# Sampled tokens of a hybrid decoder step: state step within attention, experts within the spreading, heads in the partitions

## The chip, the cores and the metric

The kernel runs on one core of a Trainium2 chip. The metric is the device time of one execution in microseconds (us); less is better. The core's engines work at the same time and wait for each other by semaphores: PE (TensorE), DVE (VectorE), ACT (ScalarE), POOL (GpSimd) and SP (SyncE, which here only starts transfers). POOL starts the gathers of rows by index.

## The reference

One decoder layer is computed for 1024 prompt tokens and for 8 sampled tokens. The sampled ones differ from the prompt in two places: each has its own cache of 512 past keys and values, in four pages, and its own recurrent state.

```
n  = rmsnorm(x);  q,k,v,...,gates = n @ w_in
oa = diff_attention(q, k_all, v_all)              # 4 heads; sampled: 512 cached keys and the own one
S  = f * S + (1 - f) outer v;  ob = q . S         # sampled: one step, 4 heads, state 128 x 128
h  = x + (sig(ga) * (oa @ wa) + sig(gb) * (ob @ wb)) @ w_out
# PEER: 8 heads; for each: top 16 of 128 keys twice, top 16 of the sums -> 16 experts
a  = gelu(expert_u[idx] . n2);  h = h + sum(w * a * expert_v[idx]);  y = rmsnorm(h)
```

Of the 16384 experts a token uses 8 x 16 = 128, with 1024 numbers in each of `expert_u` and `expert_v`.

## The kernel before

The tokens are cut in nine tiles, eight of 128 prompt tokens and one of the 8 sampled ones, in three groups, named a_ (tiles 0 and 1), b_ (2 to 4, the middle group) and c_ (5 to 7 and the sampled tile, the last group). A group runs through stages, each a function, and each stage ends with a barrier of all engines: project, attend_prompt, hgrn (the recurrence of the prompt), hgrn_out (its output: squares, norm, gate, transposes), merge and route (choice of experts). The last group has attend_sample between attend_prompt and hgrn. After it come spread (turns the choices of tiles 5 to 7 into dense weight matrices), sample_experts (the experts of the sampled tile, gathered) and dense (all experts for tiles 5 to 7, by matmul). Within a stage each engine has its own program in the written order; nothing reorders it.

Beside the stages of the groups b_ and c_ and of dense runs a side job, `Side`: the experts of tiles 0 to 4, gathered row by row. One "side token" is one of 640 steps: POOL gathers 128 rows of 8 KB (L1568), DVE makes a dot with the rows (L1647) and, two steps later, adds the second half of the rows (L1611); ACT makes the coefficient between (L1587 and L1589). A table, SHARES, says how many steps each stage takes (attend_sample 12, hgrn_out 6, route, spread and sample_experts 0, dense the rest); calls `side.dve`, `side.act` and `side.pool` stand between a stage's own steps and hand them out. A barrier also waits for POOL's gathers.

What the change touches, by lines of the kernel before:

- attend_sample (from L705). POOL gathers the keys of the 8 tokens and then their values, four pages each, into a ring of two buffers (L779), with side steps between; a buffer is free after DVE's use of the keys (`ring_free`) or PE's of the values (`v_used`). For each token PE spreads its q and k to all partitions (L794, L795), ACT copies q (L832), DVE multiplies the keys and adds them up (L854, L857), does the same with the own key (L861, L862), and then its side steps. After the eight tokens come the transposed scores (L799), max and exp, the sums of the maps (L805, L807), the weights with zeros between (L882), then PE's value loop (L809, L814), behind which stand the norm and the output.
- hgrn_out (from L1130). In the last group the sampled state comes first: `s0` is loaded, for each token PE spreads v (L1270), ACT copies it (L1211), DVE makes k outer v, the decayed state and the sum (L1239, L1240, L1242). Then 64 records of small matmuls (L1276) give the output, which is copied to `o_all` (L1249) after half of the side steps. Only then come the squares of all tiles (L1251).
- route (from L1664). For each of 8 heads DVE finds the top 16 in two lists for each tile (L1796 to L1804, eight instructions a list). The sampled tile's lists have 8 partitions. Then each tile has a "lot", from the cast L1835 to L1888: candidates, top 16 for 8 heads, index arithmetic, weights; one DMA saves the record.
- spread (from L1893). 24 batches of 16 tokens: DVE makes one-hot tiles (L1993, L1997), PE a product for each token (L1958), ACT copies four at a time (L1970); after each 8 batches the next tile's choices are transposed (L1948) and copied (L1986). SP saves 12 blocks of 2 MB.
- sample_experts (from L2002). For each sampled token PE spreads n2 (L2057), DVE makes the dot with the gathered rows (L2096), ACT gelu, PE sums the second halves (L2063); a norm and the save follow (L2104 on).

The arena's low part holds `qk` and the values of the prompt, which the last group's attend_prompt reads last.

## Time and profile before

| | us |
|---|---|
| median of 3 runs | 3947.42 (3947.03 to 3948.1) |
| profiled execution | 3950.18 |
| its span, first to last instruction | 3948.5 |
| PE busy in the span | 2897.7 (73%) |
| DVE busy | 2500.7 (63%) |
| POOL, ACT busy | 1002.2, 935.0 |

Busy time is the union of an engine's instructions. The chain of work that ended last lies with PE in dense (two lines of 16% each), but that chain is followed back only as far as the last stage's start of loading; each stage before it has a chain of its own, and the stages follow one another by barriers. The granted clock is a share of TensorE's full 2.4 GHz; it has two levels, 1.2 and 2.4 GHz, and a mean between them is a mix in time.

### The profile page before, as it was taken

To read this page: it belongs to the slowest core of one execution; us is meant where nothing else is said; L and a number is where in the kernel's file an instruction comes from. 1 tells how busy PE (TensorE), PEld (TensorE's weight loads), DVE (VectorE), ACT (ScalarE), POOL (GpSimd) and SP (SyncE) were. 2 spreads that over 40 slices of the span, in tenths; PEclk is the share of its full clock that TensorE was granted. 3 is DMA by queue.
4 is the path that set the end of the run, shared out by engine and by line. 5 is a ranking of instruction groups with operands and counts; after the bars stand their busy time and mean duration, and the time that the engine had idled before them with its cause. 6 is when DMAs were issued, how large, how long until landed. Compare 5 with 4: busy or idle time off the path is not lost. (4 is left out here: it accounts for less than half of the span.)

```text
span 3948.5 us, 30435 instructions
## 1 busy us (share of the span) xinstructions
PE 2897.7 (73%) x9486; PEld 1618.8 (41%) x9486; DVE 2500.7 (63%) x5402; ACT 935.0 (24%) x2182; POOL 1002.2 (25%) x746
## 2 busy tenths in 40 slices
PE   6748377627960975452497507789999999999998
PEld 5346243324430523212253306534555555555554
DVE  1231755774768767746487699656666666676666
ACT  1221111632211225312232016411112111121111
POOL 0000024122410441351044000023333333333332
PEclk9779698568985987666698758789999999999999
DMA  6134199458951994565498203479999999999996
GB/s 211 74 120 150 57 417 363 157 191 304 399 200 68 382 379 153 177 202 196 172 390 342 96 13 151 193 295 399 402 400 391 404 409 394 398 396 398 397 402 257
DMA packets 249536, 1075.92 MB, mean 272 GB/s; under 512 B 25024, under 2 KB 87488, under 8 KB 161936
## 3 DMA queue, kind: packets, MB, share of 16 engines
q0 software_dynamic: 99872, 704.82, 45.4%
q1 hardware_dynamic: 149504, 369.17, 24.8%
q8 instruction: 76, 1.25, 0.1%
q14 instruction: 84, 0.69, 0.1%
HBM read 1008.35 MB, written 65.55 MB: 272 GB/s over the span
## 5 line engine op out<-in xcount | busy, mean ns | idle before, releaser
L1568 POOL DMA_INDIRECT arena<-in_experts,arena x640 | 911.4, 1424 | 2012.5 <-DVE arena L1611 1993.3
L1611 DVE SCALAR_TENSOR_TENSOR arena<-arena 128x1024 f32<-128x1024 f32 x640 | 819.3, 1280 | 101.7 <-ACT arena L1589 101.4
L1647 DVE CUSTOM_DVE_ANT_0 arena<-arena 128x1024 f32<-128x1024 f32 x640 | 780.9, 1220 | 75.7 <-DMA arena<-in_experts,arena 63.0
L2176 PE MATMUL d_s_ps<-arena 128*128 128x384 f32 x2048 | 688.5, 487 | 21.2 <-DMA arena<-in_ut 21.2
L2185 PE MATMUL d_acc<-arena 128*128 128x512 f32 x1536 | 679.4, 592 | 0.0
L2176 PEld LDWEIGHTS d_s_ps<-arena 128*128 128x128 f32 x2048 | 387.5, 189 | 329.0 <-issue 81.1
L2185 PEld LDWEIGHTS d_acc<-arena 128*128 128x128 f32 x1536 | 290.9, 189 | 341.6 <-issue 307.4
L1587 ACT ACTIVATE arena<-arena 128x1 f32<-128x1 f32 x640 | 129.2, 202 | 964.4 <-DVE arena L1647 963.8
L2229 DVE TENSOR_TENSOR arena<-arena 128x384 f32<-128x384 f32 x128 | 71.7, 560 | 444.1 <-ACT arena L2207 433.1
L1589 ACT ACTIVATE arena<-arena 128x1 f32<-128x1 f32 x640 | 188.4, 294 | 20.7
L2207 ACT ACTIVATE arena<-d_s_ps 128x384 f32<-128x384 f32 x128 | 63.0, 492 | 443.5 <-PE d_s_ps L2176 443.5
L476 PE MATMUL ptc<-arena 128*128 128x392 f32 x256 | 88.8, 506 | 91.7 <-DMA arena<-in_w_t 86.2
L476 PE MATMUL ptb<-arena 128*128 128x384 f32 x256 | 90.2, 511 | 78.2 <-DMA arena<-in_w_t 67.1
L1958 PE MATMUL w_w_ps<-arena 128*128 128x128 f32 x768 | 115.2, 317 | 41.2 <-DVE arena L1993 37.9
L1958 PEld LDWEIGHTS w_w_ps<-arena 128*128 128x128 f32 x768 | 111.5, 219 | 45.2 <-DVE arena L1993 45.0
L1543 POOL DMA_DIRECT2D arena<-records_scratch x5 | 3.0, 606 | 480.9 <-POOLq L161 480.9
L1970 ACT COPY arena<-w_w_ps 128x512 f32<-128x512 f32 x96 | 98.1, 1061 | 75.3 <-PE w_w_ps L1958 75.1
L1394 PE MATMUL b_m_ps<-arena 128*128 128x384 f32 x256 | 90.4, 509 | 29.2 <-DMA arena<-in_wb 29.2
L1394 PE MATMUL c_m_ps<-arena 128*128 128x392 f32 x256 | 88.8, 501 | 28.0 <-DMA arena<-in_wb 28.0
L476 PEld LDWEIGHTS ptc<-arena 128*128 128x128 f32 x256 | 49.3, 195 | 130.9 <-issue 89.0
L2043 POOL DMA_INDIRECT arena<-in_experts,arena x8 | 7.5, 936 | 367.4 <-DVE arena L2090 365.2
L1997 DVE TENSOR_SCALAR arena<-iota,arena 128x128 f32<-128x128 f32 x384 | 100.3, 332 | 0.0
(437 smaller groups left out, 3410.7 us busy)
## 6 DMA issues: line engine op xcount, KB each, us to landing
arena<-in_ut SPq DMA_DIRECT2D x128, 512.0 KB, 12.9
arena<-in_vd SPq DMA_DIRECT2D x128, 512.0 KB, 9.7
arena<-in_w_t SPq DMA_DIRECT2D x96, 512.0 KB, 7.9
wd_scratch<-arena SPq DMA_DIRECT2D x12, 2048.0 KB, 6.3
arena<-wd_scratch SPq DMA_DIRECT2D x16, 1536.0 KB, 27.3
arena<-in_w_n SPq DMA_DIRECT2D x9, 2048.0 KB, 14.7
arena<-in_w_out SPq DMA_DIRECT2D x24, 512.0 KB, 8.4
arena<-in_w_query SPq DMA_DIRECT2D x24, 512.0 KB, 3.5
```

What stands on the lines that cost most here:

```text
L476: last = nc.tensor.matmul(pt[u][s][:, 0:n], wt[k % NW][:, d, :], xnt[:, d, a:a + n], start=(d == 0), stop=(d == KD - 1))
L1394: nc.tensor.matmul(g_ps[q % 2][x][:, 0:n], wg[u][x][:, d, :], xnt[:, d, t0:t0 + n], start=(d == 0), stop=(d == KD - 1))
L1568: pool.indirect_dma_start(out=c["ring"][:, s0 % RING, :], out_offset=None, in_=self.io["experts"], in_offset=bass.IndirectOffsetOnAxis(ap= ...
L1587: act.activation(c["dots"][:, r], c["dots"][:, r], ACT.Gelu).then_inc(self.gel_ready, 1)
L1589: act.activation(c["coef"][:, r], c["dots"][:, r], ACT.Copy, scale=self.entry(i)["w"][:, s0:s0 + 1]).then_inc(self.coef_ready, 1)
L1611: dve.scalar_tensor_tensor(out=h, in0=c["ring"][:, r, D:2 * D], scalar=c["coef"][:, r:r + 1], in1=h, op0=ALU.mult, op1=ALU.add).then_inc(s ...
L1647: dve.tensor_tensor_reduce(out=u, in0=u, in1=self.entry(i)["n2"], scale=1.0, scalar=0.0, op0=ALU.mult, op1=ALU.add, accum_out=c["dots"][:, ...
L1958: last = nc.tensor.matmul(w_ps[f % 4][:, k % 4, :], e1[n % 2][:, k, :], e2[n % 2][:, k, :], start=True, stop=True)
L1970: nc.scalar.copy(out[q % 2][:, :, k:k + 4].rearrange("p e t -> p t e"), w_ps[f % 4][:]).then_inc(four_taken, 1)
L1997: v.tensor_scalar(e2[n % 2][:, k, :], iota[:], slots[:, 2, own], slots[:, 0, own], ALU.is_equal, ALU.mult).then_inc(hot_ready, 1)
L2176: last = nc.tensor.matmul(s_ps[j % 2][:, 0:DN], us[j % NU][:, k, :], n2t[:, :, k, :], start=(k == 0), stop=(k == KD - 1))
L2185: last = nc.tensor.matmul(acc[x][:, n * 512:(n + 1) * 512], a[j % 3][:, x * P:(x + 1) * P], vs[j % NV][:, n * 512:(n + 1) * 512], start=(j ...
```

## The change

Three things, all on the sampled tokens.

1. The stage order of the last group becomes attend_prompt, hgrn, attend_sample, hgrn_out. Since the prompt's attention and recurrence are done by then, attend_sample uses the arena's low part: four of now six ring buffers and the state `s0` lie there. The state step moves from hgrn_out into attend_sample's loop over tokens, and its output into `o_all` there.
2. In route the sampled tile leaves the per-head lists. ACT puts each head's q of the 8 tokens into a block of zeros, and PE makes one product with a head and a token in each of 64 partitions, so its top 16 are two lists in all, and its lot has one head of 64 rows. Eight DMAs, one a head, save its record.
3. sample_experts is dropped as a stage; its steps stand in spread, at numbered batches. The ring has three buffers there, spread's products three PSUM banks in place of four and its transposes one in place of two.

```diff
-        for build in (project, attend_prompt, attend_sample, hgrn, hgrn_out, merge, route):
+        for build in (project, attend_prompt, hgrn, attend_sample, hgrn_out, merge, route):
...
-        for build in (spread, sample_experts, dense):
+        for build in (spread, dense):
```

attend_sample, for each token on PE, ACT and DVE, and after the loop:

```diff
                 nc.tensor.matmul(kb_ps[:], c["pick"][:, b, :], c["k_new"][:], start=True, stop=True
                                  ).then_inc(q_spread, 1)
+                if b == 0:
+                    pe.wait_ge(s_landed, 32)
+                else:
+                    pe.wait_ge(v_copied, b)
+                nc.tensor.matmul(v_ps[:].rearrange("p h d -> p (h d)"), c["pick"][:, b, :], i_s,
+                                 start=True, stop=True).then_inc(v_spread, 1)
             pe.wait_ge(s_ready, 1)
...
             last.then_inc(s_turned, 1)
+            pe.wait_ge(qz_ready, NS)
+            pe.wait_ge(new_ready, NS)
+            for h in range(H):
+                for b in range(NS):
+                    last = nc.tensor.matmul(so_ps[:, h, :], q_z[:, h, b, :], s0[:, b, h, :],
+                                            start=(b == 0), stop=(b == NS - 1))
+            last.then_inc(so_done, 1)
             pe.wait_ge(pr_ready, 1)
...
                 nc.scalar.copy(q_b[:], qb_ps[:]).then_inc(q_copied, 1)
+                act.wait_ge(v_spread, b + 1)
+                if b >= 1:
+                    act.wait_ge(kv_ready, b)
+                nc.scalar.copy(v_sb[:], v_ps[:]).then_inc(v_copied, 1)
                 side.act(b + 1, 2 * NS)
...
                 dve.wait_ge(q_used, b + 1)
+                if b == 0:
+                    dve.wait_ge(s_landed, 32)
+                v.tensor_tensor(s0[:, b], s0[:, b], bcast(f_s[:, :, b], [P, H, DV], 2), ALU.mult).then_inc(decayed, 1)
+                dve.wait_ge(v_copied, b + 1)
+                if b:
+                    dve.wait_ge(new_ready, b)
+                v.tensor_tensor(kv[:], v_sb[:], bcast(k_s[:, :, b], [P, H, DV], 2), ALU.mult).then_inc(kv_ready, 1)
+                dve.wait_ge(decayed, b + 1)
+                dve.wait_ge(kv_ready, b + 1)
+                v.tensor_tensor(s0[:, b], s0[:, b], kv[:], ALU.add).then_inc(new_ready, 1)
                 side.dve(b + 1, 2 * NS)
```

route, the list of lots and the save:

```diff
+        lots = [(n, t, P, HP) for n, t, cols in tiles] + ([(NT_, NP, NR, 1)] if g.sampled else [])
...
+                for h in range(HP):
+                    sp.dma_start(by_head[:, :, h, :], s_rest[h * NS:(h + 1) * NS]).then_inc(saved, 16)
```

spread, where a token's steps stand among the batches n (PE, then DVE):

```diff
+        asked = {3 + 2 * b: b for b in range(NS)}
+        dotted = {4 + 2 * b: b for b in range(NS)}
+        summed = {5 + 2 * b: b for b in range(NS)}
...
+                    if n in asked:
+                        token = asked[n]
+                        if token:
+                            pe.wait_ge(dots_ready, token)
+                        else:
+                            pe.wait_ge(idx_ready, 1)
+                        for x in range(2):
+                            last = nc.tensor.matmul(n2_ps[:, x * 512:(x + 1) * 512], c["pick"][:, token, :],
+                                                    n2[:, x * 512:(x + 1) * 512], start=True, stop=True)
...
+                    if n in dotted:
+                        token = dotted[n]
+                        u = ring[token % NRING][:, 0:D]
+                        dve.wait_ge(n2_spread, token + 1)
+                        dve.wait_ge(ring_landed[token % NRING], 16 * (token // NRING + 1))
```

How the instructions stand, on DVE in the loop over tokens in attend_sample. Before, one step with a side token and the next step's first instruction:

```order
L854 TENSOR_TENSOR arena<-arena 128x2048
L857 TENSOR_REDUCE arena<-arena 128x4x4 x2
L861 TENSOR_TENSOR arena<-kb_ps,arena 128x512
L862 TENSOR_REDUCE arena<-arena 128x4x2
L1647 ISA arena<-arena 128x1024
L1647 ISA arena 128x1
L1611 SCALAR_TENSOR_TENSOR arena<-arena 128x1024
L854 TENSOR_TENSOR arena<-arena 128x2048
```

After (L1138 is the former L854, L1644 and L1608 the side token):

```order
L1138 TENSOR_TENSOR arena<-arena 128x2048
L1141 TENSOR_REDUCE arena<-arena 128x4x4 x2
L1145 TENSOR_TENSOR arena<-kb_ps,arena 128x512
L1146 TENSOR_REDUCE arena<-arena 128x4x2
L1152 TENSOR_TENSOR arena<-arena,f_new 128x512
L1156 TENSOR_TENSOR arena<-arena 128x512
L1159 TENSOR_TENSOR arena<-arena 128x512
L1644 ISA arena<-arena 128x1024
L1644 ISA arena 128x1
L1608 SCALAR_TENSOR_TENSOR arena<-arena 128x1024
```

The three operations of the state (L1152, L1156, L1159), which stood at hgrn_out's start, now stand between the own key's sum and the side token.

On PE in spread, from the first tile's transposes to the second's. Before, with the sampled experts in a stage behind it:

```order
L1948 MATMUL w_t_ps<-ident,arena 128x128 x3
L1958 MATMUL w_w_ps<-arena 128x128 x128
L1948 MATMUL w_t_ps<-ident,arena 128x128 x3
L1958 MATMUL w_w_ps<-arena 128x128 x128
```

and in sample_experts:

```order
L2051 MATMUL s_t_ps<-ident,arena 128x8
L2052 MATMUL s_t_ps<-ident,arena 128x8
L2057 MATMUL s_n_ps<-arena,pick 128x512 x16
L2063 MATMUL s_acc<-arena 8x512 x16
```

After:

```order
L2019 MATMUL w_t_ps<-ident,arena 128x128 x3
L2023 MATMUL s_n_ps<-ident,arena 128x8
L2024 MATMUL s_n_ps<-ident,arena 128x8
L2033 MATMUL w_w_ps<-arena 128x128 x64
L2044 MATMUL s_n_ps<-arena,pick 128x512 x2
L2033 MATMUL w_w_ps<-arena 128x128 x32
L2044 MATMUL s_n_ps<-arena,pick 128x512 x2
L2051 MATMUL s_acc<-arena 8x512 x2
L2033 MATMUL w_w_ps<-arena 128x128 x32
L2044 MATMUL s_n_ps<-arena,pick 128x512 x2
L2051 MATMUL s_acc<-arena 8x512 x2
L2019 MATMUL w_t_ps<-ident,arena 128x128 x3
```

A sampled token's spreading of n2 (L2044) and sum (L2051) now stand behind every second batch, and the second tile's transposes (L2019) behind such a pair. The profile shows each of these matmuls as two records.

## Rows read from the trace of the kernel before

**Rows 1.** Windows, stage by stage: length, busy time (instructions), clock, DMA, GB/s.
```profile
core 0: us, PE busy (x) PEld busy (x) DVE busy (x) ACT busy (x) POOL busy (x), PEclk, DMA share, GB/s
1625.46:1789.29 163.83, 73.83 (x119) 20.35 (x119) 84.91 (x100) 17.07 (x40) 82.70 (x76) 0.61 0.55 180
1867.99:1938.76 70.77, 29.13 (x96) 13.36 (x96) 42.27 (x61) 17.09 (x30) 8.58 (x6) 0.57 0.47 171
2188.94:2365.89 176.95, 58.25 (x256) 32.92 (x256) 151.82 (x928) 21.21 (x21) 0.00 (x0) 0.65 0.10 32
2365.89:2534.45 168.56, 116.76 (x777) 112.54 (x777) 153.29 (x411) 98.13 (x97) 0.00 (x0) 0.86 0.37 154
2534.45:2592.17 57.72, 44.15 (x66) 13.44 (x66) 13.80 (x32) 5.54 (x13) 7.49 (x8) 0.65 0.37 148
2592.17:3948.50 1356.33, 1327.68 (x3584) 678.35 (x3584) 905.14 (x1201) 248.31 (x842) 481.55 (x347) 0.99 0.98 389
```

**Rows 2.** Timeline of attend_sample's key loop: start, length, instruction, idle time before it.
```profile
1633.56 2.29 DVE L854 TENSOR_TENSOR arena<-arena 128x2048 f32<-128x2048 f32 x1 [6.91 <-DMA arena<-in_cache_k,cache_rows]
...
1702.79 0.69 DVE L862 TENSOR_REDUCE arena<-arena 128x8 f32<-128x512 f32 x1
...
1704.67 1.28 DVE L1611 SCALAR_TENSOR_TENSOR arena<-arena 128x1024 f32<-128x1024 f32 x1
...
1707.35 0.59 ACT L832 COPY arena<-qb_ps 128x512 f32<-128x512 f32 x1 [2.04 <-PE kb_ps L795]
```

**Rows 3.** Timeline of attend_sample's PE, sums of the maps and first value matmul.
```profile
1720.90 1.91 PE L805 MATMUL w_ps<-sum_maps,arena 64*128 64x32 f32 x8 [2.98 <-DVE arena L877]
...
1724.97 1.91 PE L809 MATMUL as_o_ps<-arena 8*32 8x512 f32 x2 [1.96 <-DVE arena L882]
```

**Rows 4.** Value loop: POOL's gathers grouped (count, busy, mean ns, idle), then two timeline rows.
```profile
L779 POOL DMA_INDIRECT arena<-in_cache_v,cache_rows x24 | 24.4, 1015 | 20.2 <-PE as_o_ps L814 13.8 <-issue 6.4
...
1771.42 0.94 POOL L779 DMA_INDIRECT arena<-in_cache_v,cache_rows  x1 [0.30 <-issue]
...
1776.04 3.63 PE L814 MATMUL as_o_ps<-arena 128*32 128x512 f32 x8 [1.81 <-DMA arena<-in_cache_v,cache_rows]
```

**Rows 5.** Timeline of hgrn_out: the middle group's Silu, then the last group's state.
```profile
872.21 1.49 ACT L1213 ACTIVATE arena<-arena 128x1536 f32<-128x1536 f32 x1 [3.36 <-DMA arena<-gg_scratch]
...
1898.48 0.69 DVE L1240 TENSOR_TENSOR arena<-arena,f_new 128x512 f32<-128x512 f32 x1
...
1900.04 8.64 PE L1276 MATMUL c_hs_o_ps<-arena 128*8 128x128 f32 x64 [2.90 <-DVE arena L1242]
...
1909.42 2.29 DVE L1251 TENSOR_TENSOR arena<-arena 128x2048 f32<-128x2048 f32 x1
```

**Rows 6.** Windows of route on DVE: heads (last group, middle group), sampled lot.
```profile
2206.63:2288.32 81.69, 79.41 (x521) 0.77 0.10 32
1144.02:1207.02 63.00, 60.80 (x392) 0.84 0.14 42
2344.79:2363.47 18.68, 17.99 (x103) 0.50 0.04 14
```

**Rows 7.** Timeline of spread: DVE at the second tile, a batch on PE, DVE's last.
```profile
2421.20 0.56 DVE L1986 COPY arena<-w_t_ps 128x384 f32<-128x384 f32 x1 [0.91 <-PE w_t_ps L1948]
...
2509.28 4.29 PE L1958 MATMUL w_w_ps<-arena 128*128 128x128 f32 x32 [0.78 <-DVE arena L1993]
...
2519.26 2.27 DVE L1993 TENSOR_TENSOR arena<-arena,iota 128x2048 f32<-128x2048 f32 x1
2521.47 4.17 DVE L1997 TENSOR_SCALAR arena<-iota,arena 128x128 f32<-128x128 f32 x16
```

**Rows 8.** sample_experts: windows on PE (spreading n2; summing), then DVE's timeline.
```profile
2546.00:2566.00 20.00, 20.00 (x24) 0.50 0.76 318
2572.30:2583.00 10.70, 10.70 (x27) 1.00 0.00 0
...
2566.72 1.22 DVE L2096 CUSTOM_DVE_ANT_0 arena<-arena,s_n_ps 128x1024 f32<-128x1024 f32 x1 [2.19 <-PE s_n_ps L2057]
...
2584.01 1.21 DVE L2104 TENSOR_TENSOR arena<-s_acc,arena 8x1024 f32<-8x1024 f32 x1 [15.51 <-PE s_acc L2063]
```

More of the change, by code:

```diff
@@ L1205, in _ @@
         def _(act):
-            if g.sampled:
-                for b in range(NS):
-                    act.wait_ge(v_spread, b + 1)
-                    if b >= 1:
-                        act.wait_ge(kv_ready, b)
-                    nc.scalar.copy(v_sb[:], v_ps[:]).then_inc(v_copied, 1)
             act.wait_ge(gate_landed, 16 * (1 + g.sampled))
@@ L1672, in route @@
     NG = len(g.tiles)
-    tiles = [(n, t, rows(t), slice(t * P - g.t0, t * P - g.t0 + rows(t))) for n, t in enumerate(g.tiles)]
+    tiles = [(n, t, slice(t * P - g.t0, t * P - g.t0 + P)) for n, t in enumerate(g.prompt)]
+    NT_ = len(tiles)
+    NR = NS * HP
+    sampled = slice(g.np, g.np + NS)
     corners = [(0, 0, 1, 16), (16, 1, 3, 8), (40, 4, 4, 4), (56, 8, 8, 1)]
@@ L1744, in scores @@
                     pe.wait_ge(s_taken, h - 1)
-                for n, t, R, cols in tiles:
+                for n, t, cols in tiles:
                     for x in range(2):
                         half = slice(x * DH, (x + 1) * DH)
-                        last = nc.tensor.matmul(s_ps[h % 2][0:R, x, n, :], qt[h % 2][half, cols], keys[half, h, :],
+                        last = nc.tensor.matmul(s_ps[h % 2][:, x, n, :], qt[h % 2][half, cols], keys[half, h, :],
                                                 start=True, stop=True)
@@ L1758, in _ @@
                     query(h + 2)
+            if g.sampled:
+                pe.wait_ge(own_ready, HP)
+                for h in range(HP):
+                    for x in range(2):
+                        half = slice(x * DH, (x + 1) * DH)
+                        last = nc.tensor.matmul(own_ps[0:NR, x, :], q_own[half, h, :], keys[half, h, :],
+                                                start=(h == 0), stop=(h == HP - 1))
+                last.then_inc(own_done, 1)
         @block.scalar
@@ L1767, in _ @@
             side.act(HP, steps)
-            for n, t, R, cols in tiles:
+            for n, t, R, heads in lots:
+                ns = heads * TOPK
+                weights = s_rest[0:R, 1, :] if t == NP else rest[:, n, 1, :]
                 act.wait_ge(rows_cast, n + 1)
@@ L1804, in top16 @@
                         link.mark(v.max_index(where(x)[0:R, hi], best(x)[0:R, hi], spare(x)[0:R]))
-            lists = [((n, x), R) for n, t, R, cols in tiles for x in range(2)]
+            if g.sampled:
+                v.memset(q_own, 0.0).then_inc(own_clear, 1)
+            lists = [((n, x), P) for n, t, cols in tiles for x in range(2)]
             for h in range(HP):
@@ L1902, in spread @@
         e1 = [low.sb(f"e1_{u}", [P, TB, NK]) for u in range(2)]
-        e2 = [low.sb(f"e2_{u}", [P, TB, NK]) for u in range(2)]
+        ring = [low.sb(f"s_ring{r}", [P, 2 * D]) for r in range(NRING)]
+        record = low.sb("s_record", [NS, RECORD])
+        e2 = [m.sb(f"e2_{u}", [P, TB, NK]) for u in range(2)]
         by_token = [m.sb(f"by_token{u}", [P, 3, SLOTS]) for u in range(2)]
@@ L1906, in spread @@
         out = [m.sb(f"spread{u}", [P, NK, QT]) for u in range(2)]
-        t_ps = [banks.ps(f"w_t_ps{u}", [P, 3, P]) for u in range(2)]
-        w_ps = [banks.ps(f"w_w_ps{u}", [P, 4, NK]) for u in range(4)]
+        own = parts_of(record)
+        h, n2 = own["h"], own["n2"]
+        rows_f = m.sb("s_rows", [NS, SLOTS])
+        idx_s = m.sb("s_idx", [P, NS], U32)
+        w_s = m.sb("s_w", [P, NS])
+        coef_s = m.sb("s_coef", [P, NS, NS])
+        dots = m.sb("s_dots", [P, NS])
+        gel = m.sb("s_gel", [P, NS])
+        sm = m.sb("s_sm", [NS, 2])
+        t_ps = banks.ps("w_t_ps", [P, 3, P])
+        w_ps = [banks.ps(f"w_w_ps{u}", [P, 4, NK]) for u in range(NW)]
+        n2_ps = banks.ps("s_n2_ps", [P, D])
+        acc = banks.ps("s_acc", [P, D])
         landed = [top.sem(f"sw_landed{u}") for u in range(2)]
@@ L1931, in _ @@
             load(0)
+            sp.dma_start(record, io["records"][ts][0:NS, :]).then_inc(record_landed, 16)
             load(1)
```

730 lines of the change are left out of this document (349 added, 381 removed).

## Prediction

> **What bounds the kernel now.** I read the stages as windows first, since a barrier ends each: attend_sample, hgrn_out, route, spread and sample_experts of the last group and dense [rows 1]. In dense PE is busy for 1327.68 of 1356.33 us at a granted clock of 0.99 and the DMA engines for 0.98 of the time; no edit touches it. The other five hold 163.83 + 70.77 + 176.95 + 168.56 + 57.72 = 637.83 us, and in each a chain of engines decides, not one sum of busy time. So what each chain waits for is read next, line by line. The profiled execution took 3950.18 us (span 3948.5); the median of the three runs is 2.76 us lower. The sum is made against 3950.18 and then lowered by that.
>
> **The state step, moved into the key loop of attend_sample.** In hgrn_out it stands ahead of everything: the squares (L1251) start at 1909.42, 41.43 us after the stage's start at 1867.99 [rows 1, 5]. After, DVE begins with three gathered tokens. The third one's sum waits for a coefficient that ACT makes only behind the Silu of the gates. In the middle group the Silu of three tiles ends at 873.70, 6.14 us after the stage's start (872.21 less the wait of 3.36 and the table load of 1.28 that stands first: 867.57), and another table load of 1.28 follows [rows 5]; a fourth tile adds a third of 1.49, the gates' later issue about 0.5, the two small ACT steps 0.5, DVE's sum 1.28: 10.2 us. Saved: 41.43 - 10.2 = **31.2**; without that wait (0.5 for the memset and three tokens of 2.47) it would be 33.5.
> Beside keys the step costs little. From the end of L862 (1703.48) to the end of ACT's q copy (1707.94) DVE has 4.46 us, of which a side token takes 2.47, to 1705.95 [rows 2]. Three more operations of 0.7 each [rows 5] make it 4.6: 0.15 more in five steps, nothing in the two steps without a token, and the full 2.1 in the last, behind which no q waits: +2.9. If the new matmuls and copy for v got ahead of the next q, one such chain of 2.7 us would show in all eight steps: +21. They stand behind q's on PE and ACT, while PE is idle for most of a step, so I take the low end. The state's 2 MB now load beside the first keys, whose first use already waits 6.91 us for DMA [rows 2]: between 0 and 5.4 (2 MB at dense's 389 GB/s), I take +1.
> The 64 small matmuls with the new state (8.64 us [rows 5]) stand on PE ahead of L805, before which PE is idle for only 2.98 [rows 3]: +5.7, less a little as w's 1.91 may then run at the upper clock: **+5.5**.
>
> **Six buffers in place of two.** In the key loop nothing: DVE waits there for ACT's copy, not for rows [rows 2], and POOL's expert gathers, which stand between cache loads and wait for DVE's side tokens, hold POOL to about the same lead. In the value loop POOL waits 13.8 us for PE to free a buffer, and the stretch from PE's first value matmul (1724.97) to its last (1779.67) is 54.7 [rows 3, 4]. After, three loads are there when PE begins. Five remain with four expert gathers ahead of the last: 24 issues of 1.015 + 0.3 = 31.6. They start when DVE has copied the state's output (0.7) and done one token (2.47); the last landing takes 3.7 (1772.36 to 1776.04) and PE's last eight 3.63 [rows 4]: 42.1. So **-12.6**. The buffers' worth is bounded by 0 (POOL's order binds as before) and by about 16 (no issue gaps).
> A row bears on POOL here: its 24 gathers took 1.015 us in the mean while DVE did six two-input tokens beside it for the first third of the stretch [rows 4]. The Trainium skill (SBUF — State Buffer, section "SBUF: two separate sides") says that a DVE operation that holds the port shared with GpSimd shuts the other out for its whole length, so that descriptors are written late. By that rule each of some eight gathers could wait out a token's operation of 1.28, and the gain would be about 2.4; the trace shows little of it, so I stay with its mean.
> Attend_sample: +2.9 + 1 + 5.5 - 12.6 = **-3.2**.
>
> **Route.** The head phase falls from eight lists of keys to six. The middle group, with six, took 63.0 us where this one took 81.69 [rows 6]: -18.7. The sampled heads come back as two lists, 2 x 81.69/64 = +2.6; their scores are done under the last head's lists. The sampled lot of 18.68 us had 103 instructions; with one list in place of eight, 56 go. The remaining 47 would be 8.5 us at the mean 0.18; their rows are eight times shorter, and I take 6 (2.3 if all scaled, 18.68 if nothing did): -12.7. At the end eight DMAs save the record, not one. One with the barrier took from 2363.47 to 2365.89 [rows 1, 6]; eight lie between +0 and +17; SP does not wait between them, so +2.5. Route: **-26.3**.
>
> **Spread with the sampled experts.** The 57.72 us stage goes. DVE bounds spread: a batch is 2.2 + 4.17, one after the other, while PE needs 4.29 for it [rows 7]. On DVE come eight dots of 1.22 with their waits, 1.35 each [rows 8], and 1.3 of small operations: +12.1. On PE each token adds four records of 512 columns to spread n2 and four to sum: 8 x 0.43 = 3.5 at the upper clock (27 records in 10.70, overlapping at the edges), 8 x 0.83 = 6.7 at the lower (24 in 20.00 at 0.50) [rows 8]. Two batches with one token then need 12.1 of PE and 14.1 of DVE, so PE stays hidden but for two places: the transposes of the second and third tile stand behind a token's 3.5, and DVE, which waits 0.91 there today [rows 7], waits for that too: +7.0. The gathers hide: each has some four batches. The final norm chain (8.2 us from its first step to the stage's end, 2584.01 to 2592.17 [rows 1, 8]) runs beside the save of the last tile (8.81 from DVE's end at 2525.64 to 2534.45 [rows 1, 7]): +0.5. Sum -57.72 + 19.6 = **-38.1**.
>
> **Sum.** -31.2 - 3.2 - 26.3 - 38.1 = -98.8: 3851.4 for the profiled execution, and 3947.42 - 98.8 = **3848.6** for the median.
>
> **Rivals.**
> 1. PE bounds spread at its lower clock. For: at sample_experts' start and all through its n2 matmuls the clock was 0.50 and that stage's mean 0.65; a batch then takes twice 4.29, two batches and a token 23.9 against DVE's 14.1, and two without a token 17.2 against 12.7. All eight plus four pairs at 0.50 cost 96; with the mean at 0.65 (seven tenths of the time low) 67: 3916. Against: spread's mean is 0.86 today, with PE busy for 116.76 of 168.56 [rows 1], and the tokens fill its pauses.
> The Trainium skill (TensorE: Matmul & The Clock Gate, section "HAM oscillation — how this bites in real kernels") speaks for this rival: matmul bursts parted by waits fall back to half rate each time. The 0.50 in sample_experts agrees with it, the 0.86 in spread less.
> 2. The chains in attend_sample show, +21 in place of 2.9, or POOL paces the values as before and the six buffers do nothing, +12.6: 3861 to 3867, 3879 with both. For: POOL's expert gathers still stand between the loads. Against: the 13.8 us of waiting for PE.
> 3. Slower than before: dense loses clock, since it now follows another stage and PE alone bounds it. Its 1327.68 us of PE scale with the clock: 0.91 in place of 0.99 costs 117, giving 3965; under 0.92 it outweighs the rest. Against: 0.99 over the whole stage, and no pauses of PE that this change could lengthen.
>
> **How the numbers follow.** Forecast 73%, rival 2 15%, rival 1 8%, rival 3 2%, and 2% that stages overlap less than read and little is left. About 0.2%, some 8 us, is what a measurement of this kernel can tell from no change. Faster 0.96, same 0.02, slower 0.02. The range takes in the forecast's bounds below (third token unhindered -2.3, no waits at the two tiles -7, a cheaper lot -3: 3836, and 3 more for POOL) and rival 2 above: 3833 to 3879.
>
> **What would show it.** hgrn_out near 40 us, route near 151, attend_sample near 160.5, spread near 188 from barrier to barrier, sample_experts gone, and dense at 1356. Wrong would be: a granted clock well under 0.86 in spread; steps of the key loop near 13 us; PE waiting for value rows with POOL idle; DVE's idle at the two later tiles far from 4.4.

## The result, and the profile after

The changed kernel takes 3857.77 us (median of 4 runs, 3850.09 to 3859.17) against 3947.76 for the kernel before beside it: a ratio of 0.9768 (95% interval 0.9751 to 0.9785), 90.0 us less. Forecast were 98.8 less and 3848.6; the range 3833 to 3879 holds the result. The profiled execution is the fastest of the four, 3850.09.

The windows of the changed kernel, stage by stage as in [rows 1]: length, busy time (instructions) of PE, PEld, DVE, ACT and POOL, clock, DMA share, GB/s. They are attend_sample, hgrn_out, route, spread and dense of the last group.

```profile
1696.41:1861.39 164.98, 90.29 (x199) 30.57 (x199) 102.64 (x136) 20.48 (x48) 87.39 (x76) 0.64 0.61 204
1861.39:1901.36 39.97, 3.94 (x16) 3.14 (x16) 24.06 (x25) 12.16 (x22) 10.38 (x6) 0.50 0.56 198
2152.69:2304.49 151.80, 57.44 (x256) 34.94 (x256) 124.49 (x761) 18.67 (x29) 0.00 (x0) 0.68 0.11 37
2304.49:2493.56 189.07, 143.58 (x843) 116.73 (x843) 166.08 (x443) 100.24 (x109) 9.40 (x8) 0.88 0.47 182
2493.56:3848.40 1354.84, 1325.81 (x3584) 678.09 (x3584) 905.16 (x1201) 248.25 (x842) 482.83 (x347) 0.99 0.98 389
```

Against [rows 1]:

| stage | before | after | measured | forecast |
|---|---|---|---|---|
| attend_sample | 163.83 | 164.98 | +1.2 | -3.2 |
| hgrn_out | 70.77 | 39.97 | -30.8 | -31.2 |
| route | 176.95 | 151.80 | -25.2 | -26.3 |
| spread and sampled experts | 168.56 + 57.72 | 189.07 | -37.2 | -38.1 |
| sum | | | -92.0 | -98.8 |

Dense kept its length and its clock. Three of the four terms are right within 1.2 us; attend_sample is off by 4.4, to the wrong side. The profiled execution as a whole is 100.1 us under that of before: attend_prompt of the last group and what stands ahead of it, code that the change leaves as it was, ended 7.0 us earlier. Whether that belongs to the change had to be found out.

The inside of attend_sample is where the forecast missed. First DVE's multiplications of the keys (L1138 is the former L854) that waited, in the timeline of the changed kernel: start, length, instruction, idle time before it and what ended it. They are those of tokens 1, 4, 6 and 8; the last row is the memset behind the loop.

```profile
1706.64 2.29 DVE L1138 TENSOR_TENSOR arena<-arena 128x2048 f32<-128x2048 f32 x1 [7.36 <-DMA arena<-in_cache_k,cache_rows]
...
1739.57 2.29 DVE L1138 TENSOR_TENSOR arena<-arena 128x2048 f32<-128x2048 f32 x1 [1.11 <-DMA arena<-in_cache_k,cache_rows]
1761.81 2.29 DVE L1138 TENSOR_TENSOR arena<-arena 128x2048 f32<-128x2048 f32 x1 [3.38 <-DMA arena<-in_cache_k,cache_rows]
1783.97 2.29 DVE L1138 TENSOR_TENSOR arena<-arena 128x2048 f32<-128x2048 f32 x1 [0.97 <-DMA arena<-in_cache_k,cache_rows]
1794.50 0.06 DVE L1162 MEMSET arena<- 64x4 f32 x1
```

Before, DVE waited for rows at the first token only, and for ACT's copy at each of the others. Now three later steps wait for keys as well, though the ring has six buffers. POOL in the same loop shows why: the load of the fourth token's keys (L1041) is queued behind an expert gather (L1565), and that behind DVE's sum of a side token (L1608).

```profile
1728.12 2.86 POOL L1565 DMA_INDIRECT arena<-in_experts,arena  x1 [14.62 <-DVE arena L1608]
1731.28 0.95 POOL L1041 DMA_INDIRECT arena<-in_cache_k,cache_rows  x1 [0.30 <-issue]
```

POOL stood still for 14.62 us with free buffers ahead of it. Then PE's rows from the state's 64 matmuls (L1074) to the last values (L1088):

```profile
1795.84 9.14 PE L1074 MATMUL hs_o_ps<-arena 128*8 128x128 f32 x64
...
1808.11 1.04 PE L1083 MATMUL as_o_ps<-arena 8*32 8x512 f32 x2 [1.96 <-DVE arena L1176]
1809.08 12.19 PE L1088 MATMUL as_o_ps<-arena 128*32 128x512 f32 x24
...
1846.64 5.32 PE L1088 MATMUL as_o_ps<-arena 128*32 128x512 f32 x8 [2.81 <-DMA arena<-in_cache_v,cache_rows]
```

Three tokens' values are there when PE begins, as forecast; for each of the other five PE waits (0.61, 3.46, 2.90, 1.10 and 2.81), 10.9 us in all. From these rows and [rows 2 to 4] the stage divides like this:

| piece of attend_sample | before | after | change | forecast |
|---|---|---|---|---|
| stage's start to the first keys' use | 8.10 | 10.23 | +2.1 | +1 |
| key loop, to the memset behind it | 82.94 | 87.86 | +4.9 | +2.9 |
| memset to the first value matmul | 8.47 | 13.61 | +5.1 | +5.5 |
| value loop | 54.70 | 43.85 | -10.9 | -12.6 |
| rest | 9.62 | 9.43 | -0.2 | 0 |

In hgrn_out the third side token's sum waits for its coefficient, as forecast, and the squares (L1262, the former L1251) follow 10.62 us after the stage's start (10.2 were forecast):

```profile
1870.81 1.28 DVE L1608 SCALAR_TENSOR_TENSOR arena<-arena 128x1024 f32<-128x1024 f32 x1 [2.99 <-ACT arena L1586]
1872.01 2.29 DVE L1262 TENSOR_TENSOR arena<-arena 128x2048 f32<-128x2048 f32 x1
```

Route, windows of DVE as in [rows 6]: from the first list to the first lot with the sampled heads' two lists, and the sampled lot.

```profile
2170.69:2236.71 66.02, 63.62 (x408) 0.85 0.13 40
2293.20:2299.85 6.65, 5.96 (x47) 0.50 0.10 39
```

The lists were forecast at 63.0 + 2.6 = 65.6, the lot at 6. Its 47 instructions took 0.14 us each in the mean, where the 103 of before, a different mix, took 0.18. Instructions of one kind on rows of 16 in place of 128 got shorter by less than the rows: the former L1863 took 161 ns in place of 274, the former L1867 162 in place of 211.

Spread, DVE's copies of the second and third tile's choices (L2098, the former L1986):

```profile
2367.49 0.56 DVE L2098 COPY arena<-w_t_ps 128x384 f32<-128x384 f32 x1 [4.72 <-PE w_t_ps L2019]
2429.49 0.56 DVE L2098 COPY arena<-w_t_ps 128x384 f32<-128x384 f32 x1 [6.05 <-PE w_t_ps L2019]
```

Here "about 4.4" was forecast for each, from the 0.91 before the second tile [rows 7]. Before the third tile the kernel before waited longer, 2.17, and its batch of products ahead took 5.55 us, where most take 4.29. In the changed kernel that batch took 5.62, at a granted clock of 0.69, which makes up the difference between 4.72 and 6.05.

```profile
2474.51 0.56 DVE L1986 COPY arena<-w_t_ps 128x384 f32<-128x384 f32 x1 [2.17 <-PE w_t_ps L1948]
```

```profile
2419.64 5.62 PE L2033 MATMUL w_w_ps<-arena 128*128 128x128 f32 x32 [2.04 <-DVE arena L2110]
```

The first row is of the kernel before, the second of the changed one.

### The profile page after: what moved, and what is told of

Its sections match the earlier page's. It is cut to its first block and busy times, and to the rows that moved or that the text cites. A ratio compares the mean times of both kernels' runs of the same rounds, so it can differ in the third digit from the quotient of the medians.

```text
span 3848.4 us, 30261 instructions
## 1 busy us (share of the span) xinstructions
PE 2857.7 (74%) x9486; PEld 1603.9 (42%) x9486; DVE 2471.6 (64%) x5235; ACT 927.3 (24%) x2189; POOL 1009.0 (26%) x746
## 3 DMA queue, kind: packets, MB, share of 16 engines
q8 instruction: 76, 1.25, 0.1%
## 5 line engine op out<-in xcount | busy, mean ns | idle before, releaser
L1565 POOL DMA_INDIRECT arena<-in_experts,arena x640 | 918.1, 1434 | 2020.6 <-DVE arena L1608 2001.8
L1608 DVE SCALAR_TENSOR_TENSOR arena<-arena 128x1024 f32<-128x1024 f32 x640 | 819.1, 1280 | 103.9 <-ACT arena L1586 103.7
L1644 DVE CUSTOM_DVE_ANT_0 arena<-arena 128x1024 f32<-128x1024 f32 x640 | 780.6, 1220 | 74.7 <-DMA arena<-in_experts,arena 61.7
L476 PEld LDWEIGHTS ptb<-arena 128*128 128x128 f32 x256 | 50.3, 199 | 117.6 <-issue 72.6
## 6 DMA issues: line engine op xcount, KB each, us to landing
arena<-in_vd SPq DMA_DIRECT2D x128, 512.0 KB, 10.2
arena<-wd_scratch SPq DMA_DIRECT2D x16, 1536.0 KB, 29.4
```

The costliest lines, as they stand in the source:

```text
L476: last = nc.tensor.matmul(pt[u][s][:, 0:n], wt[k % NW][:, d, :], xnt[:, d, a:a + n], start=(d == 0), stop=(d == KD - 1))
L1565: pool.indirect_dma_start(out=c["ring"][:, s0 % RING, :], out_offset=None, in_=self.io["experts"], in_offset=bass.IndirectOffsetOnAxis(ap= ...
L1608: dve.scalar_tensor_tensor(out=h, in0=c["ring"][:, r, D:2 * D], scalar=c["coef"][:, r:r + 1], in1=h, op0=ALU.mult, op1=ALU.add).then_inc(s ...
L1644: dve.tensor_tensor_reduce(out=u, in0=u, in1=self.entry(i)["n2"], scale=1.0, scalar=0.0, op0=ALU.mult, op1=ALU.add, accum_out=c["dots"][:, ...
```

## The experiments

All times of runs below stand beside the kernel before on the same chip (medians 3948.53 to 3950.88), so a kernel is given by how far it lies under it; the changed kernel lay 90.0 under. Their intervals are 5 to 8 us wide to either side, so what is smaller is read from the stages of the profiled execution.

**Three parts, each alone.** The kernel before with only attend_sample, hgrn_out and the stage order changed; with only route; with only spread.

> The kernel before with the first part of the change alone: the order of the stages, attend_sample with six buffers and the state step, hgrn_out without it. My theory: the parts add, each stage has a chain of its own. In the trace of the changed kernel attend_sample is 164.96 us against 163.83 and hgrn_out 39.97 against 70.77, so -29.7 us, a median near 3918, with route, spread and sample_experts as before. Rival: the stages lean on each other (clock, transfers still running over a barrier), so that the part alone gives under 24 or over 36.

> The kernel before with route alone changed: all heads of the sampled tile in the partitions, one lot of 64 rows, eight saves. My theory: route of the last group 151.8 us against 176.95 as in the changed kernel, -25.2, a median near 3922. Rival: attend_sample and hgrn_out ahead of it set part of its start (clock, transfers), so that alone it gives under 20.

> The kernel before with the sampled experts alone put into spread. My theory: spread 189.1 us in place of 168.56 + 57.72, -37.2, a median near 3910, DVE's idle time ahead of the second and third tile's choices 4.7 and 6.0 us in place of 0.9, the clock of the stage at least as high as the 0.86 of before. Rival: spread falls to the lower clock level without the other parts, and PE bounds it: over 200 us.

They lay 30.9, 28.0 and 41.8 under the kernel before. The windows of the stages concerned (attend_sample and hgrn_out of the first; route of the second; spread of the third):

```profile
1701.81:1866.90 165.09, 91.36 (x199) 30.49 (x199) 102.64 (x136) 20.48 (x47) 87.68 (x76) 0.64 0.60 204
1866.90:1906.98 40.08, 3.94 (x16) 3.13 (x16) 24.06 (x25) 12.16 (x22) 10.38 (x6) 0.50 0.56 197
```

```profile
2189.23:2340.78 151.55, 56.53 (x256) 34.32 (x256) 124.59 (x761) 18.68 (x29) 0.00 (x0) 0.68 0.11 37
```

```profile
2366.12:2552.39 186.27, 140.99 (x843) 114.23 (x843) 166.07 (x443) 100.60 (x109) 9.48 (x8) 0.89 0.47 185
```

By stages -29.4, -25.4 and -40.0, together -94.8, against -92.0 in the whole. Read from the stages, the parts add within 3 us, and spread's clock does not fall. The medians add up to 100.7, more than the 90.0 of the whole, but with intervals of this width they can't tell whether the parts lean on each other a little. The first part's gain lies in hgrn_out alone.

**The changed kernel again**, unedited.

> The changed kernel once more, unedited, beside the next two on the same chip. In the trace of the changed kernel the five stages that the change touches were 92.1 us shorter in all than in that of the kernel before, and the stages ahead of them, whose code is the same, 7.0 shorter. My theory: the 92 are the change, the 7 are what executions differ by in the loads of the early stages. Then the stages here are again within 1.5 us of 165 (attend_sample), 40 (hgrn_out), 151.8 (route) and 188.5 (spread), and the difference of the medians lies between -90 and -95, whatever the early stages take in the one execution that is profiled. Rival: the early stages did get faster (another memory layout, other code loading), and the difference is near -99.

It lay 94.9 under the kernel before, with attend_sample 166.50, hgrn_out 40.34, route 152.16 and spread 186.01 in the profiled execution:

```profile
1702.95:1869.45 166.50, 91.69 (x199) 30.43 (x199) 102.65 (x136) 20.49 (x48) 87.99 (x76) 0.63 0.60 202
...
2312.14:2498.15 186.01, 139.90 (x843) 112.98 (x843) 166.07 (x443) 100.66 (x109) 9.38 (x8) 0.91 0.47 185
```

Its attend_sample starts at 1702.95, in place of 1696.41 in the first trace: 6.5 of the 7.0 us of the early stages are gone again, with the same code. They are what executions differ by; the change is worth 90 to 95. Spread lay 2.5 under its expected value: DVE waited 4.71 us at both tiles here, and 1.1 us less for ACT in the norm at the stage's end (1.45 in place of 2.54).

```profile
2374.54 0.56 DVE L2098 COPY arena<-w_t_ps 128x384 f32<-128x384 f32 x1 [4.71 <-PE w_t_ps L2019]
2435.21 0.56 DVE L2098 COPY arena<-w_t_ps 128x384 f32<-128x384 f32 x1 [4.71 <-PE w_t_ps L2019]
```

**Six buffers, or two.** One number changed back:

```diff
-        NRING = 6
+        NRING = 2
```

> The changed kernel with two ring buffers in attend_sample in place of six, all else as in it. My theory: beside keys six buffers bring nothing, since an expert gather on POOL stands between the loads, so the key loop gets no longer (87.9 us or some 3 less); beside values POOL waits again for PE to free a buffer, and the stretch from the first value matmul to the last is 54 to 55 us as in the kernel before, in place of 43.85: attend_sample near 174, some +8 to +11. Rival (the prediction's second): the six buffers do nothing there either, POOL's order binds, and the stage stays within 2 us of 165.

It lay 80.6 under the kernel before. Attend_sample took 175.33, and PE waited up to 6.13 us for a token's values:

```profile
1703.03:1878.36 175.33, 93.01 (x199) 30.81 (x199) 102.64 (x136) 20.50 (x48) 85.51 (x76) 0.65 0.57 192
```

```profile
1746.26 2.29 DVE L1138 TENSOR_TENSOR arena<-arena 128x2048 f32<-128x2048 f32 x1 [0.95 <-DMA arena<-in_cache_k,cache_rows]
1768.46 2.29 DVE L1138 TENSOR_TENSOR arena<-arena 128x2048 f32<-128x2048 f32 x1 [3.33 <-DMA arena<-in_cache_k,cache_rows]
...
1814.62 1.04 PE L1083 MATMUL as_o_ps<-arena 8*32 8x512 f32 x2 [1.96 <-DVE arena L1176]
...
1830.47 5.06 PE L1088 MATMUL as_o_ps<-arena 128*32 128x512 f32 x8 [6.13 <-DMA arena<-in_cache_v,cache_rows]
...
1863.66 5.32 PE L1088 MATMUL as_o_ps<-arena 128*32 128x512 f32 x8 [4.35 <-DMA arena<-in_cache_v,cache_rows]
```

The value loop is 1814.62 to 1868.98, 54.4 us, as in the kernel before, so the six buffers are worth 10.5 there. The keys are late by the same 0.95 and 3.33 with two buffers as with six (1.11, 3.38): there the four more bring nothing.

**The state step back in hgrn_out**, with the new stage order and six buffers kept (in attend_sample the state's load, saves, three DVE operations, matmuls and copy go; hgrn_out is that of before).

> The changed kernel with the state step back in hgrn_out, as in the kernel before; order of the stages and six buffers as changed. My theory: hgrn_out takes 71 to 72 us again (+31 to +32); attend_sample gives back what the step costs there: 2.3 ahead of the first keys, 5.1 ahead of the sums of the maps, and in the key loop up to 4.9, so 153 to 158 in place of 164.96. Net +20 to +25, a median near 3880. Rival: the late keys in the key loop come from POOL's order alone and stay without the step (the loop as long as now, 87.9), so attend_sample gives back only about 7 and the net is near +24; or the 2 MB of state do not delay the first keys, and they come no earlier than 10.2 us after the stage's start.

It lay 74.3 under the kernel before. Attend_sample took 151.26, hgrn_out 72.61: 18.9 more than as changed, a little under the 20 to 25 expected.

```profile
1698.73:1849.99 151.26, 69.11 (x119) 19.89 (x119) 85.12 (x100) 15.78 (x39) 82.43 (x76) 0.62 0.60 195
1849.99:1922.60 72.61, 30.02 (x96) 13.73 (x96) 42.29 (x61) 17.07 (x30) 8.58 (x6) 0.55 0.45 167
```

```profile
1707.14 2.29 DVE L1098 TENSOR_TENSOR arena<-arena 128x2048 f32<-128x2048 f32 x1 [7.23 <-DMA arena<-in_cache_k,cache_rows]
...
1739.03 2.29 DVE L1098 TENSOR_TENSOR arena<-arena 128x2048 f32<-128x2048 f32 x1 [2.02 <-ACT arena L1075]
...
1790.07 0.06 DVE L1112 MEMSET arena<- 64x4 f32 x1
```

The first keys come 8.41 us after the start in place of 10.23, so the 2 MB of state cost 1.8. And the fourth token waits 2.02 for ACT as before; the loop takes 82.93. So the late keys come with the state step, against the rival here, which put them down to POOL's order alone. It takes both.

**The side token ahead of the state operations**, DVE only:

```diff
+                side.dve(b + 1, 2 * NS)
                 if b == 0:
                     dve.wait_ge(s_landed, 32)
...
                 v.tensor_tensor(s0[:, b], s0[:, b], kv[:], ALU.add).then_inc(new_ready, 1)
-                side.dve(b + 1, 2 * NS)
```

> The changed kernel with DVE's three state operations of each step of the key loop behind the side token in place of ahead of it. My theory: the keys are late at the fourth, sixth and eighth token since the state operations hold up the side token by 2.1 us, with it POOL's expert gather, and with that the next keys queued behind it on POOL. With the token first these waits for keys (1.11, 3.38, 0.97) go: the key loop is 84.5 to 85.5 us in place of 87.9 (the steps without a token keep a wait of 2.4 for ACT's copy), attend_sample -2.5 to -3.5. Rival: the transfers themselves are slower beside the state's saves (256 KB a token), then the waits stay.

The waits for keys are gone; the sixth token waits for ACT only, and the loop (1716.63 to 1801.44) takes 84.81:

```profile
1769.69 2.29 DVE L1138 TENSOR_TENSOR arena<-arena 128x2048 f32<-128x2048 f32 x1 [2.36 <-ACT arena L1106]
...
1801.44 0.06 DVE L1162 MEMSET arena<- 64x4 f32 x1
```

So the mechanism is shown: three operations of 0.7 ahead of the side token delay it by 2.1, POOL's expert gather waits for it, and the next keys stand behind that gather. A smaller part was not in the theory. The late gather now falls beside DVE's next multiplication and takes 2.86 in place of 0.94 before the change and 1.15 here. The last gather of a token's keys ends 8.27 us after that multiplication began in the changed kernel (third token), 5.61 before the change and 5.62 here; 2.0 of the difference is the token, 0.65 the longer gathers. Attend_sample fell to 162.08. In the median it shows nothing (94.3 under the kernel before, beside 94.9): hgrn_out took 43.10 in that execution in place of 40.34, its saves landing later (ACT waits 10.20 us for the first of them, 5.23 in the changed kernel). So this edit alone has not been shown to make the kernel faster.

**POOL's expert gathers three loads later**, with the state operations where they were:

```diff
-                side.pool(n, 2 * NS)
+                if n >= 3:
+                    side.pool(n - 3, 2 * NS)
```

> The changed kernel with one edit in attend_sample: POOL issues the expert gathers of the side job three loads of the ring later than now. My theory: what limits the six buffers is not their number but the written order on POOL, where an expert gather waits for DVE's side token with the next rows queued behind it. Then DVE's waits for keys at the fourth, sixth and eighth token (1.11, 3.38 and 0.97 us) go or fall to the wait for ACT's copy (2.4 where no token stands before it), about -3; six tokens' values are there when PE begins, and the stretch from its first value matmul to its last falls from 43.85 to between 29 and 33: -11 to -15. Stage near 149, median 14 to 18 us under the changed kernel's 3857.8. Rival: POOL's own pace (1.25 us a gather) or the transfers set the time of the values; then PE still waits for rows, and the gain is 5 or less.

It lay 112.9 under the kernel before; 14 to 18 under the changed kernel's 3857.8 were expected, and it came to 19.8, in another set of runs. Attend_sample took 148.04, 16.9 less, and PE went through the values without a pause:

```profile
1699.98:1848.02 148.04, 87.20 (x199) 30.40 (x199) 102.59 (x136) 20.48 (x48) 90.06 (x76) 0.64 0.67 227
```

```profile
1808.41 1.04 PE L1084 MATMUL as_o_ps<-arena 8*32 8x512 f32 x2 [1.96 <-DVE arena L1177]
1809.38 29.37 PE L1089 MATMUL as_o_ps<-arena 128*32 128x512 f32 x64
```

The value loop is 30.3 us in place of 43.85, the key loop 84.8 in place of 87.86. POOL issues the same 76 gathers; only the place of 12 of them in its program moved. What limited the six buffers was the order on POOL, not their number and not the transfers.

**The state's small matmuls in the loop over tokens**, eight a token behind the next token's q, k and v, in place of 64 behind the scores' transposes:

```diff
+                if b:
+                    state_out(b - 1)
...
-            for h in range(H):
-                for b in range(NS):
-                    last = nc.tensor.matmul(so_ps[:, h, :], q_z[:, h, b, :], s0[:, b, h, :],
+            state_out(NS - 1).then_inc(so_done, 1)
```

> The changed kernel with PE's 64 small matmuls for the state's output (9.14 us in one row behind the scores' transposes) handed out over the loop over tokens, eight a token behind the next token's q, k and v. My theory: PE is idle there, so they cost nothing, and from DVE's last side token to the first value matmul it takes 8.5 to 9 us as in the kernel before, in place of 13.6: attend_sample -4.5 to -5.1, near 160, also beside values, since POOL's first expert gather there waits for DVE's side token behind the weights, which comes earlier by as much. Rival: the values that are late set the stage's end anyway, at a time of POOL's own, and the stage gets shorter by under 1.5.

It lay 96.4 under the kernel before; attend_sample took 160.73, 4.3 less. From the memset (1801.93) to the first value matmul (1809.51) it is 7.58 us in place of 13.61; 1.1 is given back in the value loop (44.98) and 0.8 in the key loop.

**A sampled token's steps in spread one batch later** (4, 5, 6 on in place of 3, 4, 5 on).

> The changed kernel with each of a sampled token's three steps in spread one batch later (4, 5, 6 on in place of 3, 4, 5 on), so that the batches ahead of the second and third tile's transposes have no step of a token on PE. My theory: DVE's idle time there, 4.72 and 6.05 us, is the token's four matmul pairs and falls to the 0.9 of before each: spread -8 to -9, near 180. Rival: other things delay those transposes (the one PSUM bank in place of two, which waits for DVE's copy): under -3.

It lay 97.5 under the kernel before. Spread took 179.79, 9.3 less than in the first trace and 6.2 less than in the repeat; the two idle times fell to 2.15 and 0.89:

```profile
2371.84 0.56 DVE L2098 COPY arena<-w_t_ps 128x384 f32<-128x384 f32 x1 [2.15 <-PE w_t_ps L2019]
2428.72 0.56 DVE L2098 COPY arena<-w_t_ps 128x384 f32<-128x384 f32 x1 [0.89 <-PE w_t_ps L2019]
```

That is 7.7 of the 9.3, or 6.4 against the waits of the repeat (4.71 each), which is about what it differs by. The "0.9 of before each" in the expectation holds for the second tile only; before the change the third waited 2.17. Of the rest of the 9.3, 1.1 is the wait for ACT in the final norm (1.45 here as in the repeat, 2.54 in the first trace) and does not belong to this edit.

**Five edits together, then four.** The three that helped, in hgrn_out ACT's coefficients ahead of the Silu, and in the first of the two runs the state's load behind the first keys:

```diff
+            side.act(1, 2)
             act.wait_ge(gate_landed, 16 * (1 + g.sampled))
             nc.scalar.activation(flat(gate), flat(gate), ACT.Silu).then_inc(silu_done, 1)
-            side.act(1, 2)
```

> The changed kernel with five edits: POOL's expert gathers three loads later and the state's output matmuls in the loop over tokens (attend_sample), the state's 2 MB loaded behind the first keys there, the sampled tokens' steps in spread one batch later, and in hgrn_out ACT's coefficients of the side tokens ahead of the Silu. My theory: they add up by stage. attend_sample: 148.0 with the first edit, -5 for the second, -1.5 to -2 for the third (the first keys 8.3 us after the stage's start, as without the load, in place of 10.2): 141 to 142. hgrn_out: DVE waits 2.99 us for the third token's coefficient; -2 to -3: 37 to 38. spread 179.5 to 180.5. In all about 35 us under the changed kernel beside it. Rivals: the state lands too late behind the keys (then DVE waits for it at the first token, and the third edit gives nothing or a loss), or Silu behind the coefficients becomes late for the gate's product in hgrn_out (no gain there).

It lay 121.9 under the kernel before, 27 under the changed one beside it, not 35. Most of the miss lies in attend_sample (147.61 in place of 141 to 142), and there in the state's load: the first keys came 2.0 us earlier, but DVE then waited for the state, and the key loop took 89.2.

```profile
1709.12 2.29 DVE L1144 TENSOR_TENSOR arena<-arena 128x2048 f32<-128x2048 f32 x1 [5.37 <-DMA arena<-in_cache_k,cache_rows]
1718.05 0.69 DVE L1158 TENSOR_TENSOR arena<-arena,f_new 128x512 f32<-128x512 f32 x1 [2.81 <-DMA arena<-in_state]
```

Without that edit:

> The five edits of the run before without the one that put the state's 2 MB behind the first keys. There DVE's first state operation waited 2.81 us for the state and the next 1.98 for ACT's copy of v, and the key loop took 89.2 us in place of the 84.8 of the run with POOL's gathers late, against 2.0 gained ahead of the loop. My theory: with the load in front again the loop is near 85, attend_sample near 145 (147.6 with the edit), hgrn_out near 38, spread near 179, and the median 28 to 31 us under the changed kernel's. Rival: the state's small matmuls in the loop, not the late state, lengthen it (PE's eight stand behind the next v), then attend_sample stays over 147.

```profile
1694.78:1839.81 145.03, 95.06 (x199) 32.44 (x199) 102.80 (x137) 20.66 (x48) 89.17 (x76) 0.61 0.68 232
1839.81:1878.51 38.70, 3.94 (x16) 3.14 (x16) 23.98 (x25) 12.20 (x22) 10.39 (x6) 0.50 0.59 204
```

This is the fastest kernel of the study: 3823.41 us (3816.05 to 3832.67, 5 runs), 126.6 under the kernel before, a ratio of 0.9683 (0.9667 to 0.9699). The changed kernel's was 0.9768, so by the medians the four edits are worth some 32 to 37 more, where 28 to 31 were expected; the three stages that they touch got 28 to 30 shorter (spread took 180.82). With ACT's coefficients ahead of the Silu the squares of hgrn_out begin 7.4 us after the stage's start in place of 10.62, and the stage took 1.6 to 2.4 less than 40.3 in these two runs; no run has that edit alone, and the stage's length moves by as much with the same code. The small matmuls in the loop bring less on top of POOL's order than alone (3.0 in place of 4.3 in attend_sample): the sums of the maps and the first values run at the lower clock again (granted clock 0.50, 1.91 us each in place of 1.08 and 1.04, as before the change [rows 3]), behind eight small matmuls and a wait of 1.18 in place of 64 in a row, and the value loop takes 31.4 in place of 30.3.

## Why the prediction was right, and where it was not

**hgrn_out (-31.2, measured -30.8), route (-26.3, -25.2), spread (-38.1, -37.2)** went by the steps of the text. The third side token's wait (2.99), the lists (66.02 for 65.6), the sampled lot (6.65 for 6), the eight saves (from DVE's end to the next stage 4.64 in place of 2.42: +2.2 for +2.5) and the two tile boundaries (+7.7 for +7.0, +6.3 in the repeat; the part that the run with shifted steps takes away) are each in the trace. The text took 0.91 as the wait before both tiles, but the third had 2.17, so its sum for the third, 4.4, met 4.71 in the repeat and 6.05 in the first trace, where the batch ahead ran at the lower clock in part. Where the trace of before had no row, the text gave bounds from both sides and chose a value between them: 6 for the lot of 64 rows (between 2.3 and 18.7), +2.5 for the saves (between 0 and 17). That these choices came out so near is in part luck.

**attend_sample (-3.2, measured +1.2)** failed in two terms. The first is "Beside keys the step costs little": +2.9, measured +4.9. The text had the last step right (2.1 more, measured 2.0) and counted 0.15 too much in each of five others: a step with a side token took 10.61 us before, with a wait of 2.02 for ACT, and takes 10.61 after, with none. But it took for granted that rows come as early as before, "POOL's expert gathers, which stand between cache loads and wait for DVE's side tokens, hold POOL to about the same lead". The lead is tied to the side token, and the state's three operations move that token 2.1 us later in its step. The three steps that wait for keys are 3.0 us longer for it. The run with the token first shows it: the loop takes 84.8 us, 1.9 more than before. The second is the state's load: taken as +1 between 0 and 5.4, it is +1.8 to +2.1. The value loop's -12.6 became -10.9: 1.7 of it is that PE's last eight records ran mostly at the lower clock (granted clock 0.68, 5.32 us in place of 3.63), after a wait of 2.81 for rows. Up to there the sum came out (38.5 to the last landing, forecast and measured), but two of its terms were off against each other: the 24 issues took 32.5 in place of 31.6, the last landing 2.8 in place of 3.7.

**The rivals.** Rival 1 (PE bounds spread at its lower clock) did not come: the clock was 0.88, over the 0.86 of before, and DVE waits for PE only ahead of the tiles' choices. In sample_experts the spreading of n2 ran at 0.50, 0.83 us a record [rows 8]; among the products 32 records were busy for 15.8 us, 0.49 each (PE's group in the changed kernel: count, busy, mean ns of one, which overlaps the next), at a granted clock of 1.00 for each of the eight tokens:

```profile
L2044 PE MATMUL s_n_ps<-arena,pick 8*128 8x512 f32 x32 | 15.8, 613 | 0.0
```

The Trainium skill (TensorE: Matmul & The Clock Gate, section "HAM oscillation — how this bites in real kernels") had spoken for this rival: bursts of matmuls parted by waits fall back to half rate. Here the tokens' matmuls stand directly behind the products, with no wait of their own, and did not fall. Some batches of products behind a wait of PE did in part, as the one of 5.62 us above at 0.69, which agrees with that rule; others behind the same wait of 2.04 kept 1.00 and 4.29. Only the one ahead of the third tile kept DVE waiting, for 1.3 us. Rival 2's ground, POOL's expert gathers between the loads, was real but smaller than its price: the buffers were worth 10.5 and not 0, and the order on POOL took 13.5 more of the value loop. The text weighed it as a chance of no gain; the gain that lay in moving those gathers it did not see. Rival 3 did not come: dense kept 0.99.

**The median** lies 9.2 over the forecast; 6.8 of it are the stages, 4.4 of those attend_sample. The other 2.4 is within what executions differ by: the same kernel lay 90.0 and 94.9 under the kernel before in two sets of runs. That the profiled execution itself (3850.09) lies next to the 3851.4 of the text is luck: the 7.0 us of the early stages made up for what the stages of the table lacked.

## What to carry to other kernels

A deeper ring helps only as far as the engine that fills it is free to run ahead: before counting on the buffers, read what else stands in that engine's program between two loads, and whom each of those waits for. When operations are put into another engine's idle time, look at what behind them sends a signal, since it comes later by their length though the engine's own step gets no longer. Small work moved into another stage is best put where no hand-over of that stage (here a tile's transposes) stands right behind it.

## What the runs showed of the hardware

- POOL's gathers take longer beside some of DVE's operations. Alone one takes 0.94 us; the expert gather shown above took 2.86, issued 0.25 after the first of these rows (DVE's multiplication of two operands) began. Of eight gathers beside side tokens in the changed kernel's value loop three took 1.68, 1.96 and 1.97, the others 0.94 to 0.95: 2.8 us in all.

```profile
1727.87 2.29 DVE L1138 TENSOR_TENSOR arena<-arena 128x2048 f32<-128x2048 f32 x1
...
1815.79 1.21 DVE L1644 CUSTOM_DVE_ANT_0 arena<-arena 128x1024 f32<-128x1024 f32 x1
1815.86 1.96 POOL L1041 DMA_INDIRECT arena<-in_cache_v,cache_rows  x1 [0.30 <-issue]
1818.12 0.95 POOL L1041 DMA_INDIRECT arena<-in_cache_v,cache_rows  x1 [0.30 <-issue]
1818.13 1.25 DVE L1644 CUSTOM_DVE_ANT_0 arena<-arena 128x1024 f32<-128x1024 f32 x1
```

  What sets the long ones apart is the order: each was issued 0.07 to 0.35 us after a dot (L1644) or the multiplication had begun, and ended 0.81 to 0.83 after that instruction's end. The Trainium skill (SBUF — State Buffer, section "SBUF: two separate sides") describes a port that one of the two, whichever starts first, holds for a whole instruction while the other is shut out. The long rows agree with that; the last two rows do not: a gather and a dot that starts 0.01 later run side by side, and the dot takes 1.25 in place of 1.21. Nor were the two gathers held that were issued 0.07 after the token's sum (L1608), which has two operands too, had begun. For the value loop the mean that the prediction stayed with was the better price.
- The length of hgrn_out in the last group moved between 40.0 and 43.2 us with the same code. Its last steps wait for its saves to land; what these met in the slower executions was not settled.
- Of the same code in the early stages, profiled executions differed by several us: what follows attend_prompt of the last group began between 1615.8 and 1628.1 in the kernels with the changed stage order.
